# A two-block transformer on one core: the order of weight rests, of the router's products, of the branch and of attention's maxima

## The reference, cut to what matters

```python
h = h + concat([ya, yb, yc]) @ w_out
# routed experts
xt = rms_norm(h, norm2_g)
g_logits, e_logits = xt @ rg_w + rg_b, xt @ re_w + re_b      # 4 groups, 32 experts
g_w, e_w = softmax of the best group, softmax of the best 2 of its 8 experts
for e in 32 experts:                                         # tokens that chose e
    h += ((silu(xt[tok] @ w_gate[e]) * (xt[tok] @ w_up[e])) @ w_down[e]) * weight
gate = sigmoid(rms_norm(h, ple_norm_g) @ ple_gate_w)
h = h + gate * (p @ ple_proj_w)
# ... second block: short convolution, feed-forward, attention (16 heads, causal), feed-forward
q, k, v = rope(...); o = softmax(q @ k.T) @ v; x = x + o @ w_o
```

## Time and profile before

| | us |
|---|---|
| median of 3 runs | 1106.65 (1106.39 to 1108.82) |
| the profiled execution | 1108.08 |
| its span, first to last instruction | 1106.1 |

### The profile page before, as it was taken

The page is one execution under the profiler, slowest core; times in us unless marked ns, Lnnn a source line. Parts: engine busy times, 40 slices in busy tenths (PEclk is TensorE's granted clock), DMA queues, the critical chain, the costliest instruction groups (busy, mean ns, idle before and its releaser), DMA issues.

```text
span 1106.1 us, 17277 instructions
## 1 busy us (share of the span) xinstructions
PE 1068.0 (97%) x6370; PEld 924.6 (84%) x6370; DVE 869.8 (79%) x1132; ACT 712.6 (64%) x947; POOL 136.3 (12%) x88
## 2 busy tenths in 40 slices
PE   7999979999999999999999999999999999999997
PEld 6877868778787877679999999998778879999996
DVE  5497789999999999877766777777767867876876
ACT  6676479888888887765445554454557765554543
POOL 1001100000000000012000232341200000423320
PEclk9999889999999999999999999999999999999999
DMA  9441518888888889844554545544443235546431
GB/s 370 177 153 39 180 59 331 313 341 328 341 324 339 341 328 344 316 167 176 191 196 173 184 177 185 209 164 178 171 152 115 90 140 177 209 167 228 161 142 39
DMA packets 33604, 232.62 MB, mean 210 GB/s; under 512 B 3856, under 2 KB 3984, under 8 KB 6032
## 3 DMA queue, kind: packets, MB, share of 16 engines
q1 hardware_dynamic: 32688, 229.98, 56.0%
q10 hardware_dynamic: 864, 1.93, 0.5%
HBM read 230.85 MB, written 1.05 MB: 210 GB/s over the span
## 4 chain that ended last, share of the span: by engine, by line
PE 66%; DVE 21%; ACT 6%; issue 5%; POOL 1%; DMA 0%; DVEq 0%; ACTq 0%; POOLq 0%
DVE wlo L1138 9%; PE bank L1954 9%; PE bank L1955 9%; PE bank L1956 9%; PE bank L2469 8%; PE bank L2470 8%; PE bank L2471 8%; DVE wlo L1147 3%; PE bank L2319 3%; ACT whi L524 2%; PE bank L2320 2%; DVE arena L1713 2%; DVE arena L1537 2%; PE bank L2302 2%; PE bank L2327 1%
## 5 line engine op out<-in xcount | busy, mean ns | idle before, releaser
L1138 DVE TENSOR_TENSOR wlo<-raw,whi 128x2048 fp32r<-128x2048 f32 x196 | 445.4, 2287 | 57.1 <-ACT whi L524 56.4
L524 ACT ACTIVATE whi<-raw 128x2048 fp32r<-128x2048 f32 x213 | 404.5, 1913 | 70.9 <-PE bank L1956 40.5
L2469 PE MATMUL bank<-xs,whi 128*128 128x256 f32 x896 | 251.3, 281 | 1.5 <-DVE wlo L1138 1.5
L2470 PE MATMUL bank<-xs,whi 128*128 128x256 f32 x896 | 250.2, 279 | 0.0
L2471 PE MATMUL bank<-xs,wlo 128*128 128x256 f32 x896 | 250.0, 279 | 0.0
L2469 PEld LDWEIGHTS bank<-xs,whi 128*128 128x128 f32 x896 | 168.4, 188 | 3.7 <-DVE wlo L1138 2.3
L2470 PEld LDWEIGHTS bank<-xs,whi 128*128 128x128 f32 x896 | 168.4, 188 | 0.9
L2471 PEld LDWEIGHTS bank<-xs,wlo 128*128 128x128 f32 x896 | 168.4, 188 | 0.0
L1954 PE MATMUL bank<-whi,rounded 128*128 128x512 f32 x344 | 137.1, 399 | 0.7 <-DVE wlo L1138 0.7
L1956 PE MATMUL bank<-whi,rounded 128*128 128x512 f32 x344 | 136.1, 396 | 0.0
L1955 PE MATMUL bank<-wlo,rounded 128*128 128x512 f32 x344 | 136.0, 395 | 0.0
(11 more groups left out here) (333 smaller groups left out, 1603.8 us busy)
## 6 DMA issues: line engine op xcount, KB each, us to landing
raw<-stream SPq DMA_DIRECT2D x215, 1024.0 KB, 4.8
arena<-finals ACTq DMA_DIRECT2D x3, 512.0 KB, 5.7
xres<-x_in SPq DMA_DIRECT2D x2, 512.0 KB, 4.9
raw<-stream SPq DMA_DIRECT2D x4, 256.0 KB, 6.1
out<-xn SPq DMA_DIRECT2D x4, 256.0 KB, 2.2
par<-params SPq DMA_DIRECT2D x1, 844.0 KB, 12.1
cst<-table SPq DMA_DIRECT2D x1, 502.0 KB, 8.7
arena<-p_in ACTq DMA_DIRECT2D x1, 256.0 KB, 7.3
```

Source lines behind the costliest of these rows:

```text
L524: act.activation(whi[:, s, :], raw[:, a, :], ACT.Copy).then_inc(S("high_done"), 1)
L1138: dve.tensor_tensor(wlo[:, s, :], raw[:, unit0 % RAW, :], whi[:, s, :].bitcast(F32), ALU.subtract)\
L2469: pe.matmul(o, whi[:, s, w], xhi[:, kk, :], start=first, stop=False, skip_group_check=True)
L2470: pe.matmul(o, whi[:, s, w], xlo[:, kk, :], start=False, stop=False, skip_group_check=True)
```

## The change

The router multiplies plain 32-bit numbers: the turned residual, copied without gain (`xturn`), is the stationary operand, and the router weights with the gain worked in by GpSimd (`rw`) move through it, so that the logits come with tokens on partitions. The 8 transposes of the first half of the residual stand ahead of the last piece of `w_out`. The ranking products read fp32r copies. The two subtractions for the exponentials come behind `pick_quad`, and `token_rest(1)` ahead of the keys. In a pair, the first half of unit 5's rest stands ahead of `hidden_low` of the first expert, the second half ahead of that of the second, `slot_weights` ahead of the second `hidden`, and `back_out` ahead of the second `silu_pair`. In the last two pairs unit 4's rest is halved around the first `fold`, unit 5 is rounded before the first `silu_pair`, and the rest of p is made before the pairs. The branch is passed ahead of `project(0)`, and half of `project(1)` stands ahead of `turn(3)`. In attention a ScalarE exponential stands ahead of `v_high(0)`, `maxima(0)` ahead of `v_low(0)`, `turn_heads(0)` behind one quarter of a product, and in the second run `o_high` ahead of `pt_high`, `o_low` ahead of `maxima`.

```diff
@@ -152,8 +152,8 @@
         rounded = sb("rounded", [P, 5888], F32R)
-        rhi = sb("rhi", [P, KD, NG + NE], F32R)
-        rlo = sb("rlo", [P, KD, NG + NE], F32R)
+        rw = sb("rw", [P, KD, NG + NE])
...
...
@@ -443,6 +447,8 @@
                 pe.wait_ge(S("of_normed"), TT)
+                pe.wait_ge(S("y_pair"), 2 * PAIRS)
...
...
@@ -588,7 +594,9 @@
             act.wait_ge(S("params_loaded"), 16)
-            act.activation(rhi[:], router_w, ACT.Copy).then_inc(S("piece_high"), 1)
+            act.wait_ge(S("table_loaded"), 16)
+            act.activation(strict_r, C("strict"), ACT.Copy)
+            act.activation(ones_r, C("ones"), ACT.Copy).then_inc(S("piece_high"), 1)
...
...
@@ -687,18 +695,28 @@
             turn_y_act(2)
-            split_to(U_WOUT + 5)
-            norm_act(1, slice(0, 3))
-            turn_act(2)
-            norm_act(1, slice(3, 4))
-            for t in range(TT):
+            def tokens_high(t):
...
                    .then_inc(S("xtok_high"), 1)
+            split_to(U_WOUT + 5)
+            norm_act(1, slice(0, 3))
+            for b in range(2):
+                act.wait_ge(S("turned"), 4 * 2 + b + 1)
+                act.activation(xturn[:, 2 * b:2 * b + 2, :], bank[4 + b][:].rearrange("p (k t) -> p k t", k=2),
+                               ACT.Copy).then_inc(S("xhi_ready"), 1)
+            tokens_high(0)
+            norm_act(1, slice(3, 4))
+            act.wait_ge(S("turned"), 4 * 2 + 4)
+            act.activation(xturn[:, 4:6, P:T], bank[7][:, 0:T].rearrange("p (k t) -> p k t", k=2), ACT.Copy)\
+               .then_inc(S("xhi_ready"), 2)
+            tokens_high(1)
+            split_to(U_MOE + 2)
...
             act.activation(V("eg"), V("eg"), ACT.Exp).then_inc(S("router_exp"), 1)
-            split_to(U_MOE + 2)
...
...
@@ -755,16 +773,21 @@
                 out(0)
-                silu_pair(x, 0)
-                ahead(5)
+                if x.last_quad:
+                    ahead(5)
+                    silu_pair(x, 0)
+                else:
+                    silu_pair(x, 0)
+                    ahead(5)
...
                 out(2)
+                back_out(x)
...
                 hidden_high(x, 1)
-                back_out(x)
...
...
@@ -776,11 +799,11 @@
             split_to(U_PLEG)
+            overflow_act(act)
...
             ins.then_inc(S("projected"), 1)
-            overflow_act(act)
...
@@ -980,6 +1003,8 @@
             split_to(U_QKV + 7)
+            act.activation(V("eg")[:, 0:1], Q("g0")[:, 0:1], ACT.Exp)
...
...
@@ -999,10 +1024,11 @@
                     exponentials(8 + i)
+                if i in (4, 6, 8):
+                    o_high(4 + (i - 4) // 2)
...
                     pt_high(8 + i - 1)
-                if i in (4, 6, 8):
-                    o_high(4 + (i - 4) // 2)
...
...
@@ -1044,6 +1070,10 @@
             pool.wait_ge(S("values_ready"), 1)
+            pool.wait_ge(S("gains_loaded"), 16)
+            for k in range(KD):
+                ins = pool.tensor_scalar(rw[:, k, :], router_w[:, k, :], Q("g2")[:, k:k + 1], None, ALU.mult)
+            ins.then_inc(S("router_scaled"), 1)
...
...
@@ -1263,8 +1293,6 @@
             dve.wait_ge(S("params_loaded"), 16)
-            dve.wait_ge(S("piece_high"), 5)
-            dve.tensor_tensor(rlo[:], router_w, rhi[:].bitcast(F32), ALU.subtract).then_inc(S("piece_low"), 1)
...
...
@@ -1430,11 +1458,22 @@
                 tokens_scaled(t, 1)
-            turn_dve(2)
+            dve.wait_ge(S("turned"), 4 * 2 + 3)
+            dve.tensor_copy(xturn[:, 4:8, 0:P], bank[6][:].rearrange("p (k t) -> p k t", k=4))\
+               .then_inc(S("xt_ready"), KD // 2)
+            dve.wait_ge(S("turned"), 4 * 2 + 4)
+            dve.tensor_copy(xturn[:, 6:8, P:T], bank[0][:, 0:T].rearrange("p (k t) -> p k t", k=2))\
+               .then_inc(S("xt_ready"), KD // 2)
+            def token_rest(t):
+                dve.wait_ge(S("xtok_high"), t + 1)
+                dve.scalar_tensor_tensor(xtok_lo[:, t, :], xg2[:, t, :], rstd[:, t:t + 1],
+                                         xtok_hi[:, t, :].bitcast(F32), ALU.mult, ALU.subtract)\
+                   .then_inc(S("xtok_ready"), 1)
+            token_rest(0)
             dve.wait_ge(S("router_done"), 1)
-            dve.tensor_copy(logits_t, bank[0][0:NG + NE, 0:T]).then_inc(S("logits_ready"), 1)
-            dve.wait_ge(S("logits_turned"), 1)
...
...
@@ -1442,15 +1481,9 @@
                 dve.wait_ge(S(f"rstd{t}_ready"), 2)
-                ins = dve.scalar_tensor_tensor(lg[:, t, :], bank[1][:, NR * t:NR * t + NR], rstd[:, t:t + 1],
+                ins = dve.scalar_tensor_tensor(lg[:, t, :], bank[2 + t][:, 0:NR], rstd[:, t:t + 1],
...
             link(ins)
-            def token_rest(t):
-                dve.wait_ge(S("xtok_high"), t + 1)
-                dve.scalar_tensor_tensor(xtok_lo[:, t, :], xg2[:, t, :], rstd[:, t:t + 1],
-                                         xtok_hi[:, t, :].bitcast(F32), ALU.mult, ALU.subtract)\
-                   .then_inc(S("xtok_ready"), 1)
...
@@ -1464,7 +1497,6 @@
             eg = two(V("eg"))
-            dve.tensor_tensor(eg, lg[:, :, 0:NG], over(gmax, NG), ALU.subtract).then_inc(S("router_diff"), 1)
...
...
@@ -1475,13 +1507,12 @@
             one_hot(oh2, em, v2, C("iota32"), NE, cand)
-            dve.tensor_tensor(dv, v2, v1, ALU.subtract).then_inc(S("router_diff"), 1)
-            dve.tensor_tensor(V("sel"), V("oh1"), V("oh2"), ALU.add).then_inc(S("routed"), 1)
-            token_rest(0)
+            dve.tensor_tensor(sel, oh1, oh2, ALU.add).then_inc(S("routed"), 1)
+            token_rest(1)
             dve.wait_ge(S("ranked"), 1)
-            dve.scalar_tensor_tensor(V("key"), bank[0][:, 128:192], 1.0, V("sel"), ALU.add, ALU.mult)\
-               .then_inc(S("routed"), 1)
+            dve.scalar_tensor_tensor(two(V("key")), bank[0][:, 128:192].rearrange("p (a e) -> p a e", a=TT), 1.0,
+                                     sel.bitcast(F32), ALU.add, ALU.mult).then_inc(S("routed"), 1)
...
...
@@ -1504,7 +1535,8 @@
             pick_quad(slice(0, 4), 0, S("pick_ready"))
-            token_rest(1)
+            dve.tensor_tensor(eg, lg[:, :, 0:NG], over(gmax, NG), ALU.subtract).then_inc(S("router_diff"), 1)
+            dve.tensor_tensor(dv, v2, v1, ALU.subtract).then_inc(S("router_diff"), 1)
...
...
@@ -1526,6 +1558,8 @@
             quad_weights(slice(4, 8), 1, S("wt_ready"))
+            dve.wait_ge(S("router_exp"), 3)
+            dve.tensor_tensor(plo, p_t, phi.bitcast(F32), ALU.subtract).then_inc(S("wt_ready"), 1)
...
...
@@ -1578,21 +1612,30 @@
                 ahead(3)
-                if x.p0 == PAIRS - 2:
-                    dve.wait_ge(S("router_exp"), 3)
-                    dve.tensor_tensor(plo, p_t, phi.bitcast(F32), ALU.subtract).then_inc(S("wt_ready"), 1)
+                if x.last_quad:
+                    split_part(x.unit(4), 0)
+                    fold(x, 0)
+                    split_part(x.unit(4), 1)
+                    hidden(x, 0)
+                    hidden_low(x, 0)
+                    fold(x, 1)
+                    slot_weights(x)
+                    hidden(x, 1)
+                    split_part(x.unit(5), 0)
+                    hidden_low(x, 1)
+                    split_part(x.unit(5), 1)
+                    return
...
                 hidden(x, 0)
+                split_part(x.unit(5), 0)
...
                 fold(x, 1)
+                slot_weights(x)
                 hidden(x, 1)
-                split_part(x.unit(5), 0)
+                split_part(x.unit(5), 1)
                 hidden_low(x, 1)
-                split_part(x.unit(5), 1)
-                slot_weights(x)
...
...
@@ -1874,7 +1917,7 @@
             def head(h, first):
-                if h < first + 8:
+                if first < h < first + 8:
...
...
@@ -1892,6 +1935,7 @@
             split_to(U_QKV + 7)
+            maxima(0)
...
...
@@ -1914,12 +1958,12 @@
                     over_sums(8 + i)
+                if i in (4, 6, 8):
+                    o_low(4 + (i - 4) // 2)
...
                     v_low(1)
-                if i in (4, 6, 8):
-                    o_low(4 + (i - 4) // 2)
...
...
@@ -2270,27 +2312,52 @@
             w_out(1, 1, (1, 2, 3), (0,))
+            NR = NG + NE
+            def turn_router(t, half):
+                pe.wait_ge(S(f"residual{t}_ready"), 1 + half)
+                for k in range(4 * half, 4 * half + 4):
+                    if half == 0:
+                        o = bank[4 + k // 2][:, (k % 2) * T + P * t:(k % 2) * T + P * t + P]
+                    elif t == 0:
+                        o = bank[6][:, P * (k - 4):P * (k - 4) + P]
+                    else:
+                        o = bank[(7, 0)[k // 2 - 2]][:, P * (k % 2):P * (k % 2) + P]
+                    ins = pe.transpose(o, xres[:, t, P * k:P * k + P], ident)
+                    if half == 0 and t == 1 and k % 2 or half == 1 and k == 7:
+                        ins.then_inc(S("turned"), 1)
```

(58 more changed lines are left out.)

6 lines of the change are left out of this document (3 added, 3 removed).

## The result

The changed kernel took 1097.57 us (median of 5 runs, 1094.86 to 1100.03) beside 1106.78 (1106.39 to 1108.82) of the kernel before: ratio 0.9906, 95% interval 0.9891 to 0.9921 (ratios here are estimated over all runs and are not the quotient of the two medians). On a second occasion it took 1096.49 (ratio 0.9901, 0.9886 to 0.9916). Forecast were 1094.0 and a gain of 12.6 us; 9.2 and 10.8 were measured. The profiled executions differ by 10.75 in their spans (1106.1 and 1095.35).

A forecast was written before the change was run, and what follows sets the result against it. It took the order of work between engines, not TensorE's or VectorE's own work, to bound the kernel. Router 0.9, regular pairs 4.8, last pairs and projection 3.7, attention 3.2 sum to 12.6 us: 1106.65 to 1094.0, range 1089.0 to 1100.5.

The forecast's parts named there:

- its total: Whole router stage, from logits to fetches: a gain of 0.9 us, bounds -2.9 and +2.5.
- the low level: Ranking and fetches: TensorE runs at the 1.2 GHz clock level after idling 5.23 us; when it rises decides the gain.
- The sum to the logits: Router, from the start of the transposes to VectorE's first logits: 5.8 to 6.0 us instead of 6.85, gain 0.9.
- the case for which I had said half a microsecond: Fetches: if the clock level rises at the same instant as before, early fetches run slow and 0.5 us is left.
- Rival D: Router stage: ScalarE's queue and the low clock eat all its gain and 1.7 us more, 1096.6 us; chance 0.08.
- The term of 0.34 us a pair: 14 regular pairs: the half rest fills VectorE's wait, ScalarE's rounding leaves 0.34 us free a pair; 4.8 us in all.
- the ring: Regular pairs: TensorE turns rows, VectorE folds, both pass pieces with ScalarE, next rests start late; the order bounds, not one engine.
- ScalarE is late next: Regular pairs: once 0.34 us a pair is won, VectorE's earlier start is held by ScalarE's rounding.
- Last two pairs: Last two pairs and projection: waits at turn_rows, the next unit and turn(3) shrink; 3.7 us, bounds 1.5 and 5.2.
- Attention: Attention: waits at turn_heads(0), the first turn_p and values shrink; 3.2 us, bounds 1.3 and 3.9.
- C: Regular pairs: VectorE's half rest waits for unit 5's rounding; slower from 0.9 us a pair, 1109.5 at 1.1; chance 0.07.
- a sign of being wrong: Feed-forward stages, which nothing touches: forecast unchanged, gain 0; any change there would show the prediction wrong.

The follow-up runs named there:

- e8: The changed kernel with only the first half of each row of weight units 20 to 111 loaded, so half of the pairs' weights is stale: 1096.45 us.
- e10: The kernel before with only the first half rest of unit 5 ahead of hidden_low in the regular pairs, back_out and slot_weights left at the end: 1106.46 us, ratio 0.9989.
- e2: The kernel before with only the new orders of the last two pairs and the projection, project(1) split around turn(3), branch ahead of project(0): 1104.19 us, ratio 0.9974.
- e3: The kernel before with only the router's part of the change, including the rest of p made early: 1106.46 us, ratio 0.9991.
- e4: The kernel before with only the attention part of the change: 1103.08 us, ratio 0.9957.
- e6: The changed kernel with ScalarE's four bank clearings ahead of the two exponentials instead of behind them: 1095.97 us, ratio 0.9887.
- e11: As e2, with the rest of p made ahead of the pairs instead of in the last-but-one pair: 1105.31 us, ratio 0.9980.
- e5: The changed kernel measured once more, nothing altered, to see its scatter: 1096.49 us.
- e1: The kernel before with only the regular pairs' part of the change (half rest of unit 5, back_out and slot_weights earlier): 1103.07 us, ratio 0.9967.
- e7: As e6, plus 38 products nobody reads while TensorE waits for the ranking and 10 ahead of the first fetch: 1093.26 us, ratio 0.9873.
- e9: As e7, with VectorE's second fetch copy before the weights chain's last steps, keys and pick_quad ahead of token_rest(1): 1094.77 us, ratio 0.9883.
- e12: The kernel before with 17 unread FP32 products of 128 columns while TensorE waits for the ranking and 4 ahead of the first fetch: 1105.47 us, ratio 0.9983.

## Why the prediction was right, and where not

**Router.** Right in its total, and right that the low level decides. But the total came out by two misses that cancel, which is luck. The sum to the logits was 0.4 too dear: they start at 148.95 instead of 150.28, 1.3 us earlier, or 1.5 counted from the 600th product; the products cost 3.6, not 3.8, and the copies showed no wait. By the Trainium skill ("FP8 and Floating Point Precision", TensorE Precision Notes) FP32 takes four passes; had each brought its own weight load, the router would have ended 3.8 us later, and the rows give 0.20 to 0.23 a product, so that reading is out. The level then ate the rest: it rose no earlier, the case for which I had said half a microsecond, and 0.9 was left because keys and fetches were 2.0 us earlier, not 1.45 (0.4 of that from the logits). Rival D doesn't hold.

**Regular pairs.** The term of 0.34 us a pair was right in size: 4.5 us for 14 pairs without landing waits (e8), for 4.8. Its reason was half wrong. I gave the half rest as the cause and `back_out` as a side remark; e10 shows that the half rest alone brings 0.11, since the ring closes over ScalarE's roundings. "ScalarE is late next" was right (12.8 us of waits of VectorE for line 530).

**What I left out** is the weight stream. The DMA share of 0.87 in the pairs stood in the trace of the kernel before. The change takes it to 0.91, and between 253 and 270 us, where three of the five late landings lie, to 0.97. The change doesn't create late landings: among the kernels with the pairs of before, e2 has four in its 14 pairs (3.2 us of waits), e3 two (1.7), e4 none. But in these traces they cost more. Over the shortest 14 pairs of their order (262.88; 258.37 in e8) the six executions with the old order lose 1.3 us at most, and six with the new one 0.4 to 4.0 (the changed kernel 0.9, e6 4.0). The 0.9 is most of the 1.2 that the pairs lack. Why single landings come late isn't settled.

**Last two pairs.** 3.24 for 3.7. What the rest of p brought isn't settled: the difference of 2.1 us between e2 and e11 is in good part a late unit (see e11). What is missing stands in one place, the wait of 1.01 at 452.63, which e5 has at 0.35 with a stage of 97.83. It comes from the weight stream too: `gate_up_out` stands behind the rounding of a unit that landed late. All eight executions with the new order of the last pairs have landing waits behind 440 us, 1.2 to 3.0 us in all, and the six without it none; whether they hold TensorE varies.

**Attention.** 3.5 for 3.2, independent of all else (e4). The moved table load fits ahead of `v_high`, which waits for TensorE and not for it (ScalarE's timeline after):

```profile
808.61 1.28 ACT L1007 ACT_TABLE_LOAD   x1
809.90 0.20 ACT L1007 ACTIVATE sm<-par 128x1 f32<-128x1 f32 x1
810.25 1.27 ACT L965 ACTIVATE arena_r<-bank,rstd 128x512 fp32r<-128x512 f32 x2 [0.15 <-PE bank L2000]
```

**C**, the slower side, showed itself as a trace only: VectorE waits once, 0.43 us, for the rounding of unit 5, in the pair at 266 us whose unit had landed late. It is nowhere near 0.9 in every pair.

**The untouched feed-forward stage**, whose change I had named as a sign of being wrong, did change, by 0.33 us. It is one wait of TensorE for a rest, 0.35 us at 627.45 before and 0.72 at 620.18 after. It comes with the last pairs' part: 255.5 to 255.7 us in the eight executions that have it, 255.1 to 255.3 in the six that don't. Why isn't settled.

Of the distance to 1094.0, 1.9 us are terms (1.2 pairs, 0.5 last pairs, 0.3 in the untouched feed-forward stage, less 0.3 in attention, 0.1 at the start, rounded); 1.4 is that the profiled execution before stood that much above its median and this one on it (both had the low stretch near 92 us), and 0.2 lies outside the spans (2.0 us before, 2.2 after).

## What to carry to other kernels

When a wait is taken out of a ring of engines, price the queue that closes the ring, and try each moved instruction alone: the one that looked like the cause brought a third. When the DMA engines are busy nine tenths of the time in a ring that lives on a weight stream, part of a shorter period can be lost to late landings, so count the DMA share among the bounds, and before two executions are compared at one wait, look whether a unit landed late in one of them. And where TensorE idles ahead of a short serial stage, see at which clock level the stage runs: here 0.9 of 2.0 us won inside it arrived, and keeping TensorE busy brought as much as shortening the stage did.

## What the runs showed of the hardware

The level fell 3.2 us earlier when TensorE's work ended 1.3 us earlier, and rose at nearly the same place; in four executions with the whole router part (the change twice, e3, e8) the low stretch was 13.65 us, and in e6, which has it too, 10.24; in those with the router before it was 10.24 or, in e4, 6.83, so the same router stage varies by nearly 1 us (32.20 in e4, 33.15 in e1) from one execution to the next. With products that nobody reads it was absent (e7, e9) or 3.41 us long (e12). A plain product of 36 columns, two records, takes 0.20 to 0.23 us at 2.4 GHz.
